# The gather stages of a decoder step, run in rounds with one signal from TensorE and one from VectorE in each

## What is computed

```python
q = (h @ w_q)                       # 8 heads, two halves of the key
s1, s2 = q1 @ k1.T, q2 @ k2.T       # 128 keys in each half
i1, i2, gate = top16(top16(s1) + top16(s2))   # 8 heads x 16 experts = 128 for each token
hid = gelu(h . u[i1 * 128 + i2])    # one number for each token and chosen expert
out = sum(gate * hid * v[i1 * 128 + i2])      # 128 rows of v, 1024 wide, for each token
x = x + out
```

## Time and profile before

| what | value |
|---|---|
| median of three runs | 2355.18 us |
| span of the profiled execution | 2353.7 us |
| TensorE busy | 2044.5 us (87%) |
| VectorE busy | 1177.2 us (50%) |
| GpSimd busy | 1001.2 us (43%) |
| queue of the indirect DMAs (q0) | 310.68 MB |
| first gather stage | about 723 to 1180 us |
| second gather stage | about 1918 to 2349 us |

### The profile page before, as it was taken

The page is one execution under the profiler, slowest core; times in us unless marked ns, Lnnn a source line. Parts: engine busy times, 40 slices in busy tenths (PEclk is TensorE's granted clock), DMA queues, the critical chain, the costliest instruction groups (busy, mean ns, idle before and its releaser), DMA issues.

```text
span 2353.7 us, 38380 instructions
## 1 busy us (share of the span) xinstructions
PE 2044.5 (87%) x14289; PEld 1496.2 (64%) x14289; DVE 1177.2 (50%) x3447; ACT 650.0 (28%) x977; POOL 1001.2 (43%) x874
## 2 busy tenths in 40 slices
PE   9889999999997667889898889999999986777777
PEld 4554899999995323334356346999999973233332
DVE  2554699423333533578456834997233333333333
ACT  1332244545551001112134022454555520000000
POOL 0111469830004565656514303688500026666665
PEclk9899999999998798999997989999999998888878
DMA  6473434444447999999932334244444469999998
GB/s 233 173 279 119 144 129 159 161 162 162 168 163 264 331 355 369 362 329 335 350 122 62 90 116 152 81 161 153 162 168 164 165 217 348 360 346 357 365 357 312
DMA packets 179914, 529.91 MB, mean 225 GB/s; under 512 B 22066, under 2 KB 49234, under 8 KB 179474
## 3 DMA queue, kind: packets, MB, share of 16 engines
q0 software_dynamic: 87296, 310.68, 36.3%
q1 hardware_dynamic: 91282, 216.25, 26.8%
q10 hardware_dynamic: 1152, 0.52, 0.1%
HBM read 524.69 MB, written 2.69 MB: 224 GB/s over the span
## 4 chain that ended last, share of the span: by engine, by line
PE 68%; another core or an unknown queue 8%; DVE 8%; POOL 5%; issue 5%; DMA 3%; ACT 2%; SPq 1%; DVEq 0%; ACTq 0%; PEldq 0%
PE bank L950 10%; PE bank L952 10%; PE bank L951 10%; PE bank L769 8%; PE bank L1014 8%; PE bank L990 4%; POOL u_low L703 3%; PE bank L1032 3%; PE bank L1092 2%; DVE i_one_hot L2172 2%; DMA v_slot<-in_peer_v,v_rows 2%; POOL v_slot L712 2%; PE bank L979 1%; PE bank L1242 1%
## 5 line engine op out<-in xcount | busy, mean ns | idle before, releaser
L712 POOL DMA_INDIRECT v_slot<-in_peer_v,v_rows x417 | 394.6, 946 | 703.8 <-PE bank L952 441.1
L950 PE MATMUL bank<-h_parts,u_high 128*128 128x288 f32 x2048 | 607.0, 296 | 7.9 <-POOL u_low L703 6.2
L951 PE MATMUL bank<-h_parts,u_high 128*128 128x288 f32 x2048 | 604.4, 295 | 0.0
L952 PE MATMUL bank<-h_parts,u_low 128*128 128x288 f32 x2048 | 602.8, 294 | 0.0
L950 PEld LDWEIGHTS bank<-h_parts,u_high 128*128 128x128 f32 x2048 | 384.1, 188 | 11.6 <-POOL u_low L703 9.6
L952 PEld LDWEIGHTS bank<-h_parts,u_low 128*128 128x128 f32 x2048 | 385.8, 188 | 0.0
L951 PEld LDWEIGHTS bank<-h_parts,u_high 128*128 128x128 f32 x2048 | 384.6, 188 | 0.0
L1597 ACT CAST u_high<-u_slot 128x1024 fp32r<-128x1024 f32 x256 | 268.7, 1050 | 400.5 <-PE bank L952 249.1
L703 POOL TENSOR_TENSOR u_low<-u_slot,u_high 128x1024 fp32r<-128x1024 f32 x120 | 321.1, 2686 | 93.5 <-ACT u_high L1597 93.4
L1014 PE MATMUL bank<-v_slot,weight_columns 128*32 128x512 f32 x1412 | 274.1, 687 | 57.3 <-DMA v_slot<-in_peer_v,v_rows 34.1
L1014 PE MATMUL bank<-v_slot_of_columns,weight_columns 128*32 128x512 f32 x636 | 246.2, 687 | 69.8 <-DVE weight_columns L2179 44.0
(11 more groups left out here) (393 smaller groups left out, 2463.2 us busy)
## 6 DMA issues: line engine op xcount, KB each, us to landing
u_slot<-in_peer_ut SPq DMA_DIRECT2D x256, 512.0 KB, 3.5
w_q<-in_peer_w_q SPq DMA_DIRECT2D x8, 2048.0 KB, 14.4
region<-in_cache_a_kt SPq DMA_DIRECT2D x8, 960.0 KB, 11.8
region<-in_cache_a_v SPq DMA_DIRECT2D x8, 960.0 KB, 11.4
v_slot<-in_peer_v,v_rows POOLq DMA_INDIRECT x417
region<-in_ev_w_in SPq DMA_DIRECT2D x3, 2048.0 KB, 15.1
region<-in_pool_kv POOLq DMA_DIRECT2D x40, 128.0 KB, 5.0
ckv_t_norm<-in_pool_ckv SPq DMA_DIRECT2D x64, 64.0 KB
```

The source lines that it names most:

```text
L712: pool.indirect_dma_start(out=VS[l][slot], out_offset=None, in_=v_rows, in_offset=bass.IndirectOffsetOnAxis(ap=IDX[:, at:at + 1], axis=0)) ...
L950: pe.matmul(bank, uh, HR[:, 0, c, :], start=(c == 0), stop=False)
L951: pe.matmul(bank, uh, HR[:, 1, c, :], start=False, stop=False)
L952: ins = pe.matmul(bank, ul, HR[:, 0, c, :], start=False, stop=(c == KC - 1))
```

## The change

The gather stage is put in rounds, 76 in each layer (`ROUNDS`). In round r TensorE spreads group r, picks group r-2 and multiplies group r-4, and then counts up one semaphore, `round_multiplied`. VectorE's answer to round r is the weights of group r-2 and then the one-hot of group r, and it counts up `round_weighed`. TensorE begins round r when VectorE has answered round r-2. The waits of GpSimd, SyncE and ScalarE for picks and values are put in rounds too (`picked`, `valued`): a pick of group g is over at the end of round g+2, its values at the end of round g+4. The places of `key_norms` move one or two rounds, the `s5_turns` of VectorE two. The order in which GpSimd issues its DMAs, and their slots, are the same. The four signals of `key_sums` become one of four. The work on the last tile stands behind the loop.

```diff
@@ -49,10 +49,12 @@
 NVS = 9
 GROUPS = [("sample", q) for q in range(NS // 4)] + [(t, j) for t in range(2) for j in range(32)]
 NGR = len(GROUPS)
-
-
-NORM_PLACES = ([(q, third) for q in range(29, 39) for third in (0, 1)]
-               + [(q, third) for q in range(43, 72) for third in (0, 1, 2) if third < 2 or q % 3 == 1][0:60])
+PICK_LAG, VALUE_LAG = 2, 4
+ROUNDS = NGR + VALUE_LAG
+
+
+NORM_PLACES = ([(q, third) for q in range(30, 40) for third in (0, 1)]
+               + [(q, third) for q in range(45, 74) for third in (0, 1, 2) if third < 2 or q % 3 == 1][0:60])
 NORM_STEP = {place: n for n, place in enumerate(NORM_PLACES)}
 NORM_ENDS = [NORM_PLACES[20 * k + 19][0] for k in range(4)]
 
@@ -66,6 +68,16 @@
 
     kind, j = g
     return [SEQ + 4 * j + i for i in range(4)] if kind == "sample" else [P * kind + 32 * i + j for i in range(4)]
+
+
+def picked(l, groups):
+
+    return ROUNDS * l + groups + PICK_LAG
+
+
+def valued(l, groups):
+
+    return ROUNDS * l + groups + VALUE_LAG
 
 
...
@@ -541,12 +553,12 @@
                     load(US[e % 4], I["peer_ut"][l, e], f"u_loaded{e % 4}")
                 if l == 0 and live(3):
 
-                    sp.wait_ge(sem("picked_full"), NS // 4)
+                    sp.wait_ge(sem("round_multiplied"), picked(0, NS // 4))
                     load(S5P[:, 0:3, :], I["s5_par"], "gain0_then_s5_par_loaded")
...
                 tokens = [t for g in GROUPS for t in group_tokens(g)]
                 for t, (slot, signal, count, _) in zip(tokens, V_PLAN[l]):
 
-                    pool.wait_ge(sem(signal), before_layer[signal] + count)
+                    if signal == "hidden_full":
+                        pool.wait_ge(sem("hidden_full"), l * NK + count)
+                    elif signal == "s5_factors_made":
+                        pool.wait_ge(sem("s5_factors_made"), count)
+                    else:
+                        pool.wait_ge(sem("round_multiplied"), picked(l, count) if signal == "picked" else valued(l, count))
                     at = hidden_column(t)
                     pool.indirect_dma_start(out=VS[l][slot], out_offset=None, in_=v_rows,
                                             in_offset=bass.IndirectOffsetOnAxis(ap=IDX[:, at:at + 1], axis=0)).then_inc(sem(f"v_loaded{slot}"), 16)
@@ -968,27 +984,18 @@
                     pe.matmul(bank[:, :], ZEROS, X[:, 1, 0:512], start=True, stop=False, skip_group_check=True)
 
                 def spread_i1(q):
-                    n = l * NGR + q
                     kind, j = GROUPS[q]
-                    if n >= 2:
-
-                        pe.wait_ge(sem("one_hot_ready"), n - 1)
                     for i in range(4):
                         out = banks[q % 2][:, i * P:i * P + P]
                         at = ident32[:, 4 * j + i:4 * j + i + 1] if kind == "sample" else ident16[:, 4 * j + i:4 * j + i + 1]
                         ins = pe.matmul(out, at.broadcast_to([P, P]), I1B[:, 2 if kind == "sample" else kind, :], start=True, stop=True)
-                    ins.then_inc(sem("i1_spread"), 1)
+                    return ins
 
                 def pick(q):
-                    n = l * NGR + q
-                    pe.wait_ge(sem("one_hot_ready"), n + 1)
-                    if n >= 2:
-
-                        pe.wait_ge(sem("weights_ready"), n - 1)
                     for i, t in enumerate(group_tokens(GROUPS[q])):
                         out = banks[2 + q % 2][:, i * P:i * P + P].rearrange("p (b r) -> p b r", r=ROWS)
                         ins = pe.matmul(out, OH1[:, q % 2, i, :], HID[:, :, hidden_column(t), :], start=True, stop=True)
-                    ins.then_inc(sem("picked_full"), 1)
+                    return ins
 
                 def values(q):
                     kind, j = GROUPS[q]
@@ -997,7 +1004,6 @@
                         pe.wait_ge(sem("x_tile_updated"), 6 * l + 4)
                         clear(banks[4])
                         clear(banks[5])
-                    pe.wait_ge(sem("weights_ready"), l * NGR + q + 1)
                     slots = []
                     for slot, _, _, landing in V_PLAN[l][4 * q:4 * q + 4]:
...
@@ -1038,8 +1044,9 @@
                         pe.wait_ge(sem("key_vars"), k)
                     pe.wait_ge(sem("key_squares"), 16 * k + 4 * m + 4)
                     for i in range(4):
-                        pe.matmul(banks[7 if k else 5][32 * i:32 * i + 32, :], SUMW[:, m, :], KSQ[k // 2][:, i, :], start=(m == 0), stop=(m == 3),
-                                  skip_group_check=True).then_inc(sem("key_squares_used"), 1)
+                        ins = pe.matmul(banks[7 if k else 5][32 * i:32 * i + 32, :], SUMW[:, m, :], KSQ[k // 2][:, i, :], start=(m == 0), stop=(m == 3),
+                                        skip_group_check=True)
+                    ins.then_inc(sem("key_squares_used"), 4)
 
                 def key_norms(q, third):
 
                     clear(banks[k])
-                for q in range(NGR + 2):
-                    if q < NGR:
-                        spread_i1(q)
-                    key_norms(q, 0)
-                    if 1 <= q <= NGR:
-                        pick(q - 1)
-                    key_norms(q, 1)
-                    if l == 0 and q == NGR + 1:
-
-                        pe.wait_ge(sem("weights_ready"), NGR)
+                for r in range(ROUNDS):
+                    if r >= PICK_LAG:
+
+                        pe.wait_ge(sem("round_weighed"), (NGR + PICK_LAG) * l + r - PICK_LAG + 1)
+                    if r < NGR:
+                        ins = spread_i1(r)
+                    key_norms(r, 0)
+                    if PICK_LAG <= r < NGR + PICK_LAG:
+                        ins = pick(r - PICK_LAG)
+                    key_norms(r, 1)
+                    if l == 0 and r == ROUNDS - 1:
+
                         odd_norm(0)
                         odd_norm(1)
-                    if q >= 2:
-                        values(q - 2)
-                    key_norms(q, 2)
+                    if r >= VALUE_LAG:
+                        ins = values(r - VALUE_LAG)
+                    ins.then_inc(sem("round_multiplied"), 1)
+                    key_norms(r, 2)
 
 
             pe.wait_ge(sem("ident_then_w_in1_loaded"), 16)
...
@@ -2157,29 +2167,18 @@
                 say("zeros_ready")
 
                 def one_hot(q):
-                    n = l * NGR + q
-                    dve.wait_ge(sem("i1_spread"), n + 1)
-                    if n >= 2:
-
-                        dve.wait_ge(sem("picked_full"), n - 1)
-                    dve.tensor_scalar(OH1[:, q % 2].rearrange("p i k -> p (i k)"), banks[q % 2][:, :], pcol, None, ALU.is_equal).then_inc(sem("one_hot_ready"), 1)
+                    dve.tensor_scalar(OH1[:, q % 2].rearrange("p i k -> p (i k)"), banks[q % 2][:, :], pcol, None, ALU.is_equal).then_inc(sem("round_weighed"), 1)
 
                 def weights(q):
-                    n = l * NGR + q
                     toks = group_tokens(GROUPS[q])
-                    dve.wait_ge(sem("picked_full"), n + 1)
                     for i, t in enumerate(map(hidden_column, toks)):
                         step(dve.scalar_tensor_tensor(out=OH1[:, q % 2, i, :], in0=iota, scalar=I2T[:, t:t + 1], in1=banks[2 + q % 2][:, i * P:i * P + P],
                                                       op0=ALU.is_equal, op1=ALU.mult, accum_out=ACTC[:, q % 2, i:i + 1]))
                     settle()
-                    if q >= 4:
-
-                        dve.wait_ge(sem("v_used"), n - 3)
                     at = hidden_column(toks[0])
-                    dve.tensor_tensor(WZ[:, 4 * (q % 4):4 * (q % 4) + 4, 31], ACTC[:, q % 2, :], GT[:, at:at + 4], ALU.mult).then_inc(sem("weights_ready"), 1)
-
-                def add_tile(t, last):
-                    dve.wait_ge(sem("v_used"), l * NGR + last + 1)
+                    return dve.tensor_tensor(WZ[:, 4 * (q % 4):4 * (q % 4) + 4, 31], ACTC[:, q % 2, :], GT[:, at:at + 4], ALU.mult)
+
+                def add_tile(t):
                     if t == 2:
                         for g in range(4):
                             x = X[0:NS, 2, 256 * g:256 * g + 256]
@@ -2190,21 +2189,20 @@
                             TT(x, x, banks[6 - 2 * t + h][:, :], ALU.add)
+                    dve.wait_ge(sem("round_multiplied"), ROUNDS * l + q + 1)
+                    if q >= PICK_LAG:
+                        ins = weights(q - PICK_LAG)
+                        if q < NGR:
+                            step(ins)
+                            settle()
+                        else:
+                            ins.then_inc(sem("round_weighed"), 1)
                     if q < NGR:
                         one_hot(q)
-                    if 1 <= q <= NGR:
-                        weights(q - 1)
-                    if l == 0 and q == NGR + 1:
-                        odd_var(0)
-                        odd_var(1)
-                        odd_scale(0)
-                        odd_scale(1)
```

(17 more changed lines are left out.)

27 lines of the change are left out of this document (13 added, 14 removed).

## The result

The kernel after took 2375.16 us (median of 4, 2368.8 to 2380.19), the kernel before beside it 2355.34 us (2349.54 to 2357.84). The ratio is 1.0091, its 95% interval 1.0068 to 1.0115: slower, where 2331 us had been forecast. A second comparison gave 1.0105 (1.0070 to 1.0140).

The account below looks back on a forecast made before the run. It took a loop of late signals between TensorE, VectorE and GpSimd as the bound, not the transport. Terms -18 -9 +4.7 -2 = -24 us gave 2331 us; own range 2315 to 2345, with rivals 2288 to 2380.

Parts of the forecast that it names:

- The handshake in the second layer: Second gather stage: TensorE's 46.4 us of waits for weights go, a group takes 5.60 us instead of 5.90; 18 us saved.
- The first layer: First gather stage: 0.15 us saved for each of 58 groups, 9 us; ends 0 and 29.
- the loads that hang on picks: Load of S5's parameters, hanging on pick 8 and wanted one round later: costs nothing, or 2 us at most.
- VectorE's further work: First gather stage: VectorE's own other work fills 34.7 of 40 us in one stretch, unchanged, so little can be won.
- The starts: Start of each gather stage: first values in round 4, not 2; 4.7 us lost over two layers, bounds nothing and 2 x 5.
- The ends: End of each gather stage: one pick gone from behind the last landing; 2 us saved in two layers, or nothing.
- The increments of a semaphore: TensorE's signals: two fewer in each of 144 rounds, about 26 ns each, 7.6 us saved at most; not added.
- A: The transport is the bound already: nothing won in the middle, 4.7 us lost at the starts; 2358 us, chance 0.18.
- C: The single signal, told after the values, is late and lengthens the rounds' period, 6.5 us at 7.4 late; 2394 us, chance 0.19.
- B: Transport holds 397 GB/s in the second stage, first layer gains half a microsecond a group; 2291 us, chance 0.13.

Follow-up runs that it names:

- once-filled kernels: Kernels before and after, each slot filled once a stage and read again, most transfers left out: 2043.2 and 2048.1 us.
- split_fixed: Kernel after with TensorE's three signals back, first twenty key-norm steps a round later, VectorE's key variances and scales a round earlier: 2352.1 us, 1.0031.

## Why the prediction was wrong

- **The handshake in the second layer, -18 us: this step failed.** It took 46.4 us of waits for weights as the cause of the pace. They were a symptom. The waits went (46.4 to 0) and a group takes what it took: 417.9 us before and 418.4 after from values 0 to 71. Half the bytes, small products and 13 slots left the pace where it was as well (5.8 to 6.1 us a group). The once-filled kernels show that the handshake before needed no time beyond TensorE's own 3.13 us when signals are prompt; with late ones it wasn't tried alone. The transport kept 357 GB/s, the least that the prediction allowed, where its sum had taken 373.
- **The first layer, -9 us: wrong in sign.** Values 0 to 71 took 10.6 us longer.
- **An omitted term.** The diff moves the first key-norm step from round 29 to 30, while the values move by two rounds. So it stands ahead of values 26, not 27. The prediction gave this no term. It is the larger stall, +11.3 us, of which 5.3 came back with the place alone. For the loads that hang on picks the prediction allowed 2 us at most for the single signal; with three signals the standstill ahead of the first key projection was 7.7 us and not 12.7, though TensorE also came to it 5 us later.
- **VectorE's further work "in the same order and of the same size": true, but priced at nothing.** VectorE's variances now come behind its answer to a whole round, and TensorE waited 5.5 us for them. The stall is 8.1 us; with these variances a round earlier it was gone from the profile, though not from the timed ratio.
- **The starts, +4.7: too small.** Measured +5.1 and +3.1 at the first values, 8.2 together and within the bound of 2 x 5. The first was regained by group 24, the second was kept.
- **The ends, -2: not seen.** Values 56 to 71 took 2.1 us less in the first stage and 0.3 us more in the second, and no experiment isolates the last round.
- **The increments of a semaphore.** TensorE's three signals given back made the kernel 8 to 11 us faster, not slower. The Trainium skill ("TensorE: Matmul & The Clock Gate", section "The cost: per-tile semaphore tail") counts only what an increment costs the sender, some 26 ns; no run here isolates that price. That the receivers lose more by hearing later is the likely reading, argued from what the edit changes.

Of the rivals, A came nearest for the middle of the second stage: 357 GB/s before and after, and only the start lost (+3.1 us). Its 2358 us lacked the two stalls and the price of the single signal. Its reason, a transport full by bytes, is refuted by the half rows. The Trainium skill ("DMA: Bandwidth & Descriptors", section "Where 436 GB/s comes from") has some 358 GB/s as a core's share of the memory; in the long condition, with full rows, the windows of 300 us and more are near it (357 to 364), in the short condition 409 GB/s stood for 300 us, so the trace doesn't agree with it as a fixed limit. C's mark is there (TensorE waits for the one-hot ahead of the spreads) and its cause is in part (the single signal costs 8 to 11 us), but its longer period is not: the second stage keeps its pace at a DMA share of 0.97. B never showed as an effect of the change; a rate over its 397 GB/s did stand for 300 us, in the short condition.

Still open is what makes a group of four indirect transfers take 5.9 us in one condition and 5.2 in another. It isn't half of the bytes, the size of the products, four slots or TensorE's waits for weights. Three rivals are left: the number of transfers, which was the same in all these kernels; the late signals, which the kernels in the form of before had with the gather in the long condition (medians of 2.5 to 6.3 us) and not in the short one; and a common cause of both outside this core, such as traffic of others on the chip, which these traces don't hold. A smaller share of the memory's rate alone would not explain it, since the pace is the same at 180 GB/s. Nor is it a difference between chips: the sets with 2268.9 and 2354.4 us ran on the same one.

As to the 20 us lost: with the two places put right and the signals given back the ratio went from 1.0091 (1.0068 to 1.0115) to 1.0031 (1.0011 to 1.0052), so these three together are most of it, and 5 us are left with the lags and VectorE's order. No version of the change beat the kernel before; split_fixed came nearest.

## What to carry to other kernels

A wait that ends last in the profile need not be what sets the pace: before pricing its removal, take the work away that would be late next, and see whether the pace moves. When a pipeline's lag is changed, list everything that is placed by round number (side work, load triggers, another engine's follow-up) and shift each with the stage that it must not hold up. Merging signals makes every receiver hear as late as the last; here that cost more than it saved.

## What was not expected of the hardware

- One program had two conditions: 5.2 us a group, 409 GB/s and a one-hot 0.04 us behind the spread's shown end, or 5.86 us, 364 GB/s and 6.3 us (medians), with small value products in both.
- Half the bytes in the same number of transfers: DMA share 0.63 and not 0.97, and 5.8 to 6.1 us a group.
- Without transfers TensorE was busy for 180.00 of 180.00 us at the full granted clock (1.00, 2.4 GHz). With them the clock in the windows of the second stage was 0.85 to 0.97 of it with full products, and 0.63 and 0.65 with small ones.
